# Attention: both heads' scores of a row block, then values, then both turns, on TensorE

## The reference, cut to what matters

```
for blk in range(S // Q_BLOCK):                  # 8 blocks of 128 rows
    q0, q1 = blk * Q_BLOCK, (blk + 1) * Q_BLOCK
    s = (einsum('bqhd,bkhd->bhqk', q_nope[:, q0:q1], k_nope[:, :q1])
         + einsum('bqhd,bkd->bhqk', q_rope[:, q0:q1], k_rope[:, :q1])) * scale
    s = where(k_chunk[None, :] <= q_chunk[:, None], s, -inf)   # chunks of 64
    prob = softmax(s, axis=-1)
    outs.append(einsum('bhqk,bkhd->bqhd', prob, v[:, :q1]))
```

## Time and profile before

| what | value |
|---|---|
| median of three runs | 2051.26 us |
| the profiled execution, its own time | 2051.6 us |
| its span, first to last instruction | 2049.9 us |
| attention: the stretch read below | 267 to 538 us, 271 us for 8 pairs |
| granted TensorE clock in it | 1.00 of full |
| busy in it: TensorE, weight load, VectorE, ScalarE | 262, 215, 169, 145 us |

### The profile page before, as it was taken

One profiled execution on the slowest core, in us unless ns is written; L12 is line 12 of the kernel. 1 busy time (PEld: TensorE's weight loads), 2 busy tenths in 40 slices (PEclk: granted clock), 3 DMA queues, 4 the chain that ended last, 5 costly groups with the idle time before them and its releaser, 6 DMA issues. The chain is left out here.

```text
span 2049.9 us, 31303 instructions
## 1 busy us (share of the span) xinstructions
PE 1922.3 (94%) x11958; PEld 1361.9 (66%) x11958; DVE 782.4 (38%) x1437; ACT 669.2 (33%) x1486; POOL 614.1 (30%) x658
## 2 busy tenths in 40 slices
PE   7999999999999999999999989999989889798896
PEld 7998878787787777888887767767653233233232
DVE  5224256666553554440112356656521121111114
ACT  5334145555323344331122333333213222222222
POOL 2236387342120110001104576656212122122110
PEclk9999999999999999999999999999999899999988
DMA  7204451211321146523342422121389999999998
GB/s 255 96 32 175 135 195 27 52 27 47 144 72 39 42 80 118 102 54 97 104 103 93 173 82 74 63 73 47 123 348 417 425 425 424 425 424 425 424 424 359
DMA packets 103114, 371.39 MB, mean 181 GB/s; under 512 B 18752, under 2 KB 41664, under 8 KB 76096
## 3 DMA queue, kind: packets, MB, share of 16 engines
q1 hardware_dynamic: 85088, 327.32, 44.3%
q0 software_dynamic: 16704, 42.10, 5.4%
q10 hardware_dynamic: 1184, 0.04, 0.0%
HBM read 325.24 MB, written 60.95 MB: 188 GB/s over the span
## 5 line engine op out<-in xcount | busy, mean ns | idle before, releaser
L2880 PE MATMUL ps<-w_gu,rows_t 128*64 128x512 f32 x1024 | 241.0, 626 | 22.1 <-DMA w_gu<-w_up 20.5
L2880 PEld LDWEIGHTS ps<-w_gu,rows_t 128*64 128x64 f32 x1024 | 74.7, 144 | 163.7 <-issue 140.8
L2899 PE MATMUL ps<-w_d,act_tt 128*64 128x512 f32 x512 | 126.7, 640 | 25.2 <-DMA w_d<-w_down 24.6
L3175 POOL DMA_INDIRECT y_d<-y_out,asg_i x32 | 32.4, 1012 | 368.9 <-DVE y_out L2984 349.4
L2323 PE MATMUL ps<-w_o,mix_t 128*128 128x512 f32 x256 | 123.1, 609 | 0.0
L2975 DVE SCALAR_TENSOR_TENSOR act_g<-ps,rs_c,act_g 128x256 f32<-128x256 f32 x32 | 15.5, 483 | 278.7 <-ACT act_g L2966 278.7
L1110 ACT ACTIVATE prob<-ps,stats 128x1024 f32<-128x1024 f32 (+7 forms) x128 | 94.4, 738 | 62.7 <-DVE stats L1073 62.3
L322 PE MATMUL ps<-tk_lo,h_hi 128*128 128x512 f32 x256 | 99.9, 390 | 0.0
L322 PE MATMUL ps<-tk_hi,h_hi 128*128 128x512 f32 x256 | 99.7, 389 | 0.0
L322 PE MATMUL ps<-tk_hi,h_lo 128*128 128x512 f32 x256 | 99.7, 389 | 0.0
L1073 DVE TENSOR_REDUCE stats<-ps 128x1 f32<-128x1024 f32 (+7 forms) x128 | 97.0, 757 | 4.7 <-DVE ps L1071 0.3
(11 more groups left out here) (481 smaller groups left out, 4429.9 us busy)
## 6 DMA issues: line engine op xcount, KB each, us to landing
w_gu<-w_gate SPq DMA_DIRECT2D x64, 1024.0 KB, 23.5
w_gu<-w_up SPq DMA_DIRECT2D x64, 1024.0 KB, 25.9
w_d<-w_down SPq DMA_DIRECT2D x64, 1024.0 KB, 21.4
w_tk<-w_in SPq DMA_DIRECT2D x5, 2048.0 KB, 17.3
proj_d<-tok_o POOLq DMA_DIRECT2D x40, 256.0 KB, 2.3
tk_in<-proj_d SPq DMA_DIRECT2D x8, 1280.0 KB, 6.0
w_ch<-w_in SPq DMA_DIRECT2D x12, 512.0 KB, 9.1
proj_d<-conv_o POOLq DMA_DIRECT2D x12, 512.0 KB, 4.0
```

What stands on the lines that cost most here:

```text
L2880: mm = pe.matmul(ps[half, 2, :].rearrange("p (g n) -> p g n", g=2), rows_t[:, k, half], w_gu[q][:, h, :, k, :], start=(k == 0), stop=(k == ...
L2899: mm = pe.matmul(ps[half, 4 + j, :], act_tt[:, k, half], w_d[q][:, h, k, j * BANK:(j + 1) * BANK], start=(k == 0), stop=(k == 1))
L3175: pool.indirect_dma_start(out=y_d, out_offset=bass.IndirectOffsetOnAxis(ap=idx, axis=0), in_=y_out[q][:, :], in_offset=None, bounds_check= ...
```

## The change

Two slots of TensorE's stream become one step. It now issues the scores of both heads, then the values of the block two places back, then the turns of both heads of the block one place back. Every instruction and its semaphores stay; VectorE, ScalarE, GpSimd and the DMA queues keep their own order. The order for a block is scores 2x, scores 2x+1, values x-2, turns 2x-2, turns 2x-1.

```diff
-            def slot(u, p, j, prev):
+            def two_slots(u, p, j, prev):
                 if j < NJ:
                     scores(u, p, j)
-                x = back(u, j, 2, prev)
-                if x and x[1] < NJ:
-                    turn(*x)
+                    scores(u, p, j + 1)
                 x = back(u, j, 4, prev)
-                if x and x[1] % 2 == 0:
+                if x:
                     values(x[0], x[1] // 2)
+                for i in (j, j + 1):
+                    x = back(u, i, 2, prev)
+                    if x and x[1] < NJ:
+                        turn(*x)
 
             def pair(u, m, p, prev):
                 pe.wait_ge(s_qk, parts_made(u))
-                for j in range(NJ):
-                    slot(u, p, j, prev)
+                for j in range(0, NJ, 2):
+                    two_slots(u, p, j, prev)
 
             def tail(u):
-                for j in range(NJ, NJ + 3):
-                    slot(u, None, j, True)
+                for j in range(NJ, NJ + 4, 2):
+                    two_slots(u, None, j, True)
```

## The result

The changed kernel takes 2110.04 us (median of 5, 2108.81 to 2112.65) against 2051.31 us before (5 runs): a ratio of 1.0287, 95% interval 1.0276 to 1.0299. It is 58.7 us slower; the forecast was 2104 us, +53. The profiled execution has 2108.81 us of its own time, 57.2 more than the profiled one of before.

A forecast was written before the change was run, and what follows sets the result against it. TensorE's stream was taken to bound the kernel. New waits of 9.0 us a pair, 72 for eight, 71 after the first pair's 0.9, less 17.8 of old waits, net +53 us: 2104 us, range 2076 to 2121 us.

The forecast's parts named there:

- scores behind the exponential behind the turns: At scores 4, 8, 12 and the next pair's 0: a chain of 1.70 us each, 4.8 us bare a pair.
- turns behind turns: Blocks 7 to 4: the second head's turns wait for bank 4 to be copied out, 3.4 us bare a pair.
- scores 7, 11, 15: These scores wait for an exponential queued behind the second turns: 0.2 us each, 0.6 a pair, bounds 0 and 1.2.
- values behind a late copy: Values behind small turns whose copy waits behind the long exponential: 0.2 us at one or two places, bounds 0 and 0.5.
- The kinds: TensorE's changes between scores, turns and values, five entries becoming three: taken as 0, bounds -8.5 and +6 us.
- The old waits: TensorE weight loads' waits for other engines in the attention before: they go, covered by scores and values, -17.8 us.
- The 0.9 us that "falls out": First pair: no earlier exponential in front of its slot 0, so one wait of 0.9 us is absent, 72 becoming 71.
- The range of the case: The forecast's own range from shorter handovers, the kinds and the small terms: 2090 to 2118 us.
- Only the exponential's wait: Rival: the bank-4 copy is hidden and only the exponential waits cost, 45 less 17.8, giving 2079 us; chance 0.06.
- only the copy's: Rival: scores do not need the exponential and only the bank waits cost, +27 - 17.8, giving 2061 us; chance 0.02.
- Faster: Rival: longer scores cover the old waits and fewer changes of kind save time, -17.8 - 8.5, giving 2025 us; chance 0.04.
- The clock: Rival: the granted clock falls once in a pair during the attention, +27 us, giving 2131 us; chance 0.11.

The follow-up runs named there:

- Experiment 4: Changed kernel with the first head's turns back directly behind its scores (scores, turn, scores, values, turn): 2039.78 us, 0.9945 of the kernel before.
- experiment 6: Changed kernel with values between the two heads' turns only where the turns are those of small blocks 0 to 3: 2075.52 us.
- experiment 5: Changed kernel with values between the two heads' turns only where the turns are those of large blocks 4 to 7: 2086.22 us.
- experiments 1, 2 and 6: Changed kernel with values behind both turns, 2065.5 us; with values between the two heads' turns in every step, 2049.06 us; the third is experiment 6.

## Why the prediction came out right

The sign, the place and both mechanisms were as forecast, and so was the size to 6 us. By the steps of the prediction, for one pair:

| term | predicted | measured | from |
|---|---|---|---|
| scores behind the exponential behind the turns | 4.8 | 4.9 | four chains, below |
| turns behind turns | 3.4 | 3.5 | 1.53 each, less 0.82, 0.71, 0.60, 0.49 of own turns |
| scores 7, 11, 15 | 0.6 | 1.1 | below |
| values behind a late copy | 0.2 | 0.25 | 395.75 instead of 395.50 |
| sum | 9.0 | 9.75 | |

*The chains.* Timeline of the changed kernel, the other three places:

```profile
403.29 0.66 PE L988 MATMUL ps<-consts,prob 128*128 128x128 f32 x4
405.04 0.44 PE L322 MATMUL ps<-k_lo,q_hi 96*128 96x384 f32 x1 [1.10 <-ACTq L1116]
...
413.55 0.87 PE L988 MATMUL ps<-consts,prob 128*128 128x128 f32 x6
415.30 0.50 PE L322 MATMUL ps<-k_lo,q_hi 96*128 96x512 f32 x1 [0.88 <-ACTq L1116]
...
423.96 1.09 PE L988 MATMUL ps<-consts,prob 128*128 128x128 f32 x8
425.81 0.30 PE L322 MATMUL ps<-k_lo,q_hi 96*128 96x128 f32 x1 [0.76 <-ACTq L1116]
```

They last 1.75, 1.75 and 1.85 us, with the first one's 1.75, for a forecast of 1.70. That the chain is nearly as long everywhere, since longer turns stand before shorter exponentials, held too. In the run with four buffers both heads' turns at these four places take 0.33, 0.41, 0.63 and 0.85 us with no wait behind them; less these, 1.42 + 1.34 + 1.12 + 1.00 = 4.9 us are bare.

*The step that was mis-sized* is the estimate of 0.2 us each for the scores of slots 7, 11 and 15. Slot 11 in the changed kernel, timeline:

```profile
409.13 0.47 PE L322 MATMUL ps<-k_lo,q_hi 96*128 96x512 f32 x1
...
410.65 0.47 PE L322 MATMUL ps<-k_lo,q_hi 96*128 96x512 f32 x1 [0.23 <-ACTq L1116]
```

These are 1.52 us for 1.14 us of products: 0.38 us. The other two give 0.23 and 0.48 (1.53 us, less 1.30 and 1.05). The sum, 1.1, lay inside the bounds of 0 to 1.2. I had worked out the chain behind block 6's turns as "about 2.1 us, beside 0.7 + 1.1", which leaves 0.3, and then put 0.2. Here the chain is 2.23 us (turns at 408.42, scores at 410.65) beside 0.71 + 1.14 of own turns and scores. So the working was right to 0.1 us, and rounding it down made most of the miss; over eight pairs the term is 4 us too small.

*The kinds* were costed at nothing, between -8.5 and +6. The changed pair without its waits is 41.1 - 9.75 = 31.35 us; the one before, by the idle time of its weight loads, is 33.8 - 2.2 = 31.6. The difference of 0.25 us, 2 us in all, is about as large as the error of the reading. So the three entries in place of five brought little or nothing. The 0.17 us gaps follow the values, as the earlier trace rows had them, and now stand in front of the turns behind them (391.52 to 392.76 is 1.24 us for twenty instructions, as before).

*The old waits* of 17.8 us were taken to go because scores and values now stand in front. For one of them the reason is wrong. Seven of the 15 waits called `ACT prob` in the earlier trace rows, about 1 us each, are the turns of slot 3, and the earlier trace rows show these waiting for bank 4's copy (340.26 to 340.94, turns at 341.09). That wait did not go; it is the second new wait at block 7, which was there already, with the values of block 0 and one short set of scores between. The sum holds, since the forecast counts it whole afterwards. Of the rest, the turns' wait for ScalarE's copies (5.0 before) no longer stands in the changed kernel's rows. Experiment 4, with the new waits covered, is 11 us faster than the kernel before.

*The ends.* The 0.9 us that "falls out" did not. In the last pair no scores follow the fourth chain, but the values of block 3 do, and they wait for a copy that stands behind the same exponential on ScalarE:

```profile
590.45 1.09 PE L1003 MATMUL ps<-prob_t,v_all 128*64 128x128 f32 x16 [1.48 <-ACT prob_t L1047]
```

And the values' old wait of 1.1 us at the very end is still there. From the starts of slot 2's scores, the first pair is 7.1 us longer than before, each of the next six 7.3, and the last one with its end 7.2. With the measured pair terms the recorded sum is 8 x 9.75 - 0.9 - 17.8 = +59; with the two ends it is +62, and with the 2 us of the kinds +60, for 58.1 in the attention. What is left is within the reading's error of 0.25 us in a pair.

*The range of the case* was given as 2090 to 2118 us. Its own parts, -6, -8.5 and -6 from 2104, add up to 2083 at the lower end. Nothing else was worked out from that bound.

*The rivals.* Only the exponential's wait or only the copy's: each alone is a part, 34.5 us by experiment 6 and 23.8 us by experiment 5, so both fall. Faster: it needed the chain to be covered, and what stands between the turns and the next scores is what decided, since with values there (experiments 1, 2 and 6) most of that wait went. The clock: 1.00 over the whole attention, though TensorE was busy for 269 of 329.5 us and idle for 0.8 to 1.3 us in each chain. The Trainium skill, page "TensorE: Matmul & The Clock Gate", section "A second HAM failure mode: psum-queue depth-cycling", holds that many short idles can make the clock swing; here 80 such waits of up to 1.3 us (48 of the scores, 32 of the turns) did not, and the measurement decides for this kernel.

## What to carry to other kernels

When instructions are regrouped on the engine that sets the time, do not begin by counting entries and switches. Ask first, for every wait of the other engines (a buffer to be overwritten, a bank to be freed), how much work of the bounding engine lies between the instruction that ends it and the instruction that needs its outcome. A two-buffer rule that cost nothing in one order (0.4 us, inside the interval) cost 31 us in another that has the same instructions; the place of one filler, the values, was worth 44 to 61 us. Two instructions of one kind that share a bank or a buffer want something between them, so alternate kinds as long as the switch itself costs less than the wait it covers (0.17 us here, against the 0.7 to 1.4 us that lay bare).

## What was not expected of the hardware

- In the handover turns, exponential, scores of 1.75 us, the exponential of 1024 keys is only 1.11. The rest is the turn's modelled duration (0.27), the start of ScalarE (0.18, where the prediction's row had 0.12), the sum's read-out (0.09 beyond the exponential) and the release (0.10).
- Taking one wait away lengthened another that looked fixed: with four buffers the time from block 7's first turns to its second ones went from 1.53 to 2.09 us, since TensorE arrived before VectorE had emptied its queue.
- The engine that a wait is put down to can be the wrong one of several: slot 15's turns waited for VectorE's copy (end 429.05, turns 429.20), and the row names ScalarE, whose exponential for them had ended at 427.33.
